# Attention maps combined before they are turned, latent heads and keys made in pairs, and small steps placed between output chunks

## The chip, the cores and the metric

One core of one Trainium2 chip. The metric is the device time of one execution in microseconds; the kernel is launched once and computes everything in fp32.

## The reference

One inference step of a two-layer network for 128 context tokens and 128 latent tokens (D = 1024). Each layer has a token mixer and a mixture of 64 experts. Cut to what the change touches:

```python
# differential attention, 4 heads of 32+32: for each head
a = softmax(q1 @ k1.T * scale) - lam * softmax(q2 @ k2.T * scale)
o_d = a @ v                                   # (tokens, 64) a head; then rmsnorm over the 64
# latent attention, 8 heads
kv = ckv_all @ w_ukv                          # k_nope and v of every head, 64 + 64
s = q_nope @ k_nope.T + q_rope @ k_rope.T
o_m = softmax(s * scale) @ v                  # (tokens, 64) a head
# retention, 4 heads, in both directions; its output is gated by silu(rg)
mix = concatenate([ret_out, diff_out, mla_out], -1)     # 256 + 256 + 512
x = x + gate1 * (mix @ w_out)
x = x + gate2 * moe_ffn(h)                    # 64 experts, top 6, and a shared one
```

## The kernel before

The activations lie turned in SBUF: xT, hT and mixT have channels on the partitions and the 256 tokens (128 context, 128 latent) in the free dimension. Instructions are written by hand for every engine, in one order that is fixed by the text, and the engines wait for each other by semaphores (names in `S[...]`). The order of the code in the block of an engine is therefore the order of its queue.

A layer is: norm, mixer, norm, experts. The weights of the mixer arrive in pieces of up to 2 MB through a ring of four slots (`gu`): SyncE issues the load of piece n when piece n - 4 is used (`weights_used`). Pieces are five of w_in, w_uq and w_ukv together (`mla`), two of w_out, the shared expert's, and pieces of w_ada, the modulation, which are multiplied at the places that `ADA_AT` names (16 of 2 MB in layer 0, 8 in layer 1) and gathered in `rada`. After the mixer the 64 experts go through 22 rounds a layer, 3 MB of weights for each expert. TensorE's block takes the ada pieces up as small matrix products (`ada`), and after each four a selection (`ada_select`), whose result VectorE adds up (`ada`, L975).

Attention runs in six units i a layer (`UNITS`). Units 0, 1, 2 are differential: 0 is all heads of the context (8 maps of 128 keys), 1 and 2 are two heads each of the latent tokens (4 maps of 256 keys). Units 3, 4, 5 are latent attention: 3 the context's 8 heads, 4 and 5 four heads each with 256 keys. A map lies with the queries on its partitions. The steps of a unit are:

- scores (TensorE, L1541 or L1551), into the two PSUM banks of the unit;
- `negated_max` (VectorE, L1031), then `exps` (ScalarE, L764), which leave the exponentials in `prob` and their sums;
- `turns` (TensorE, L1555): eight 128 x 128 transposes of `prob`. All transposes of the mixer have the line of the helper `turn`, L1440;
- `even_half` (VectorE, L1039) and `odd_half` (ScalarE, L771) copy the turned maps to `probT`;
- `values` (TensorE, L1577): eight products with the turned map as the stationary weights and 64 columns of values moving through;
- `results` (VectorE, L1043): reciprocals of the sums, the scaling (L1052 or L1056), and for the differential units the subtraction of the second maps with `nlam`, squares and their sums. `o_done` frees the banks.

Latent keys: L1667, one product for each of eight heads, 64 wide weights (w_ukv) and 384 columns moving, each into partitions 0 to 63 of a bank of its own; ScalarE copies each (L834). Behind them come three products for the values, `vm` (L1675).

The mixer's end on TensorE is, in order: the last ada piece, `ada_select` (L1458, waits for `rada`), the retention's cross products (`ret_x`, L1722), four turns of keys (`t_k`), `turn_mix` for the blocks 1, 2 and 3 of `mix` (each four turns; block 1 is the differential heads', 2 and 3 the latent heads'), the retention's products (`ret_o`, L1747), its state (`kv_p`, L1753), and the output projection `project_out` (L1762), in eight chunks c of 128 output channels, each a sum over eight k blocks of `mixT`. Block 0 of `mix`, the retention's, is ready last, so its turns stand between chunks. A norm's sum over the partitions (L1484) is a product with a matrix of ones, and four idle products (L1493) follow it.

The profile gives an fp32 product as two instructions.

## Time and profile before

| what | value |
|---|---|
| median of 3 runs | 1385.82 us (1382.41 to 1386.05) |
| the profiled execution | 1387.04 us, its span 1385.2 us |
| TensorE, matmul busy | 1256.7 us (91%) |
| VectorE, ScalarE busy | 276.8 us (20%), 233.9 us (17%) |
| DMA queue q1, share of 16 engines | 86.9%, 492.68 MB |
| mean granted TensorE clock | 0.965 of full |
| layer 0: mixer with its norm, experts | about 33 to 206 us, 232 to 703 us |
| layer 1: mixer with its norm, experts | about 703 to 872 us, 898 to 1385 us |

Times in the views are microseconds from the span's start. The 1.84 us between the span and the time of the execution lie outside the profile. An engine's busy share is an average over stages with different limits, so the stages are read one by one.

### The profile page before, as it was taken

How to read it: one execution, taken by the hardware profiler on the slowest of the kernel's cores; microseconds unless marked ns; L12 is line 12 of the kernel's file. 1: busy time of each engine (PE TensorE's matmuls, PEld its weight loads, DVE VectorE, ACT ScalarE, POOL GpSimd, SP SyncE). 2: the span in 40 equal slices, each digit the busy share in tenths (PEclk: the TensorE clock that was granted, in tenths of full speed). 3: DMA queues.
4: the chain of work that ended last, by engine and by line, in shares of the span. 5: the costliest groups of instructions: out<-in, count | busy, mean ns of one | idle time of the engine just before them, and what ended most of it. 6: DMA issues, size and time to landing. Idle time of an engine off the chain costs nothing.

```text
span 1385.2 us, 22873 instructions
## 1 busy us (share of the span) xinstructions
PE 1256.7 (91%) x9680; PEld 860.7 (62%) x9680; DVE 276.8 (20%) x696; ACT 233.9 (17%) x516; POOL 2.7 (0%) x13
## 2 busy tenths in 40 slices
PE   4999999999998898888999999999999789888976
PEld 2566687667666565646565668766767465555644
DVE  2142244111110110101033424511011010101012
ACT  2143213110100000000133421311000001000101
POOL 0000000000000000000000000000000000000000
PEclk9999999999999999999999999999999999999998
DMA  9886639899999999999956554899999999999990
GB/s 391 343 337 252 267 128 407 354 421 421 420 421 421 421 423 422 422 422 421 396 190 254 206 200 160 366 367 418 421 421 420 421 422 422 422 421 423 421 409 35
DMA packets 81025, 496.16 MB, mean 358 GB/s; under 512 B 10560, under 2 KB 12864, under 8 KB 24640
## 3 DMA queue, kind: packets, MB, share of 16 engines
q1 hardware_dynamic: 76752, 492.68, 86.9%
q10 hardware_dynamic: 4208, 2.52, 0.6%
q8 instruction: 52, 0.85, 0.2%
q14 instruction: 13, 0.11, 0.0%
HBM read 493.17 MB, written 2.00 MB: 357 GB/s over the span
## 4 chain that ended last, share of the span: by engine, by line
PE 67%; DMA 28%; DVE 2%; SPq 1%; ACT 1%; issue 1%; DVEq 0%; ACTq 0%
DMA dn<-in_exp_w_down 18%; PE PS L1909 14%; PE PS L1938 12%; PE PS L1503 8%; PE PS L1841 7%; PE PS L1848 7%; DMA gu<-in_exp_w_gate 5%; PE PS L1762 4%; DMA gu<-in_w_in 2%; PE PS L1440 2%; PE PS L1807 2%; PE PS L1471 2%; DMA gu<-in_w_ada 2%; PE PS L1577 1%; PE PS L1885 1%
## 5 line engine op out<-in xcount | busy, mean ns | idle before, releaser
L1909 PE MATMUL PS<-gu,arena 128*32 128x256 f32 (+1 forms) x3072 | 319.6, 383 | 1.8 <-issue 1.8
L1909 PEld LDWEIGHTS PS<-gu,arena 128*32 128x32 f32 (+1 forms) x3072 | 187.4, 118 | 79.8 <-issue 19.8
L1938 PE MATMUL PS<-arena 128*64 128x512 f32 (+1 forms) x336 | 174.3, 667 | 60.8 <-DMA dn<-in_exp_w_down 59.3
L1938 PE MATMUL PS<-dn,arena 128*32 128x512 f32 (+1 forms) x688 | 182.1, 631 | 0.0
L1841 PE MATMUL PS<-arena 128*128 128x128 f32 x1408 | 176.3, 278 | 0.5 <-ACT arena L923 0.5
L1841 PEld LDWEIGHTS PS<-arena 128*128 128x128 f32 x1408 | 164.1, 192 | 17.9 <-issue 16.7
L1848 PE MATMUL PS<-arena 128*128 128x256 f32 x704 | 159.6, 380 | 1.4 <-ACT arena L905 1.4
L1909 PE MATMUL PS<-arena 128*64 128x256 f32 (+1 forms) x672 | 151.9, 379 | 0.0
L1848 PEld LDWEIGHTS PS<-arena 128*128 128x128 f32 x704 | 130.4, 190 | 19.8 <-ACT arena L905 3.2
L1358 DVE TENSOR_TENSOR arena<-arena,PS 128x256 f32<-128x256 f32 x44 | 18.5, 421 | 564.1 <-ACT arena L919 564.1
L905 ACT ACTIVATE arena<-PS 128x512 f32<-128x512 f32 x88 | 52.6, 597 | 458.5 <-PE PS L1938 458.5
L1938 PEld LDWEIGHTS PS<-arena 128*64 128x64 f32 (+1 forms) x336 | 43.4, 140 | 112.7 <-issue 109.9
L1909 PE MATMUL PS<-xh,arena 128*64 128x256 f32 x352 | 86.8, 403 | 25.0 <-DMA gu<-in_exp_w_gate 21.2
L1909 PEld LDWEIGHTS PS<-arena 128*64 128x64 f32 (+1 forms) x672 | 83.4, 124 | 20.4
L1909 PEld LDWEIGHTS PS<-xh,arena 128*64 128x64 f32 x352 | 49.3, 145 | 64.0 <-DMA gu<-in_exp_w_gate 25.0
L1938 PEld LDWEIGHTS PS<-dn,arena 128*32 128x32 f32 (+1 forms) x688 | 47.4, 126 | 45.6 <-issue 42.8
L1352 DVE COPY arena<-PS 128x512 f32<-128x512 f32 x44 | 30.4, 691 | 214.5 <-PE PS L1440 214.5
L919 ACT ACTIVATE arena<-PS 128x256 f32<-128x256 f32 x44 | 16.9, 384 | 325.1 <-PE PS L1909 325.1
L1503 PE MATMUL PS<-gu,xh 128*128 128x512 f32 (+1 forms) x192 | 66.0, 498 | 1.5 <-DMA gu<-in_w_in 1.5
L1503 PE MATMUL PS<-xh,gu 128*128 128x256 f32 x256 | 58.2, 388 | 3.0 <-DVE xh L1006 1.7
L1503 PEld LDWEIGHTS PS<-xh,gu 128*128 128x128 f32 x256 | 49.2, 194 | 12.4 <-DMA gu<-in_w_in 4.0
L1762 PE MATMUL PS<-xh,gu 128*128 128x256 f32 x256 | 56.1, 380 | 0.0
(232 smaller groups left out, 989.1 us busy)
## 6 DMA issues: line engine op xcount, KB each, us to landing
gu<-in_exp_w_gate SPq DMA_DIRECT2D x106, 1024.0 KB, 16.3
gu<-in_exp_w_up SPq DMA_DIRECT2D x86, 1024.0 KB, 17.6
dn<-in_exp_w_down SPq DMA_DIRECT2D x86, 1024.0 KB, 18.3
gu<-in_w_ada SPq DMA_DIRECT2D x24, 2048.0 KB, 10.8
arena<-in_exp_w_up SPq DMA_DIRECT2D x42, 1024.0 KB, 14.8
arena<-in_exp_w_down SPq DMA_DIRECT2D x42, 1024.0 KB, 16.8
xh<-in_exp_w_gate SPq DMA_DIRECT2D x22, 1024.0 KB, 11.3
gu<-in_w_in SPq DMA_DIRECT2D x8, 2048.0 KB, 12.6
```

The costliest lines, as they stand in the source:

```text
L905: return A(yy[:, :, half], PS[:, 7 - n, :].rearrange("p (t c) -> p c t", c=NC_), ACT.Copy)
L1352: return v.tensor_copy(turned_back, PS[:, 6, :])
L1358: tt(hh, sact, PS[:, 5, FF:2 * FF], ALU.mult).then_inc(S["hid_ready"], 1)
L1440: return pe.transpose(dst, src, ident[0:parts, 0:parts])
L1471: ins = mmul(PS[32 * j:32 * j + 32, 7, :], condw[:, 2 * quarter + c, :], wv[:, c, 512 * j:512 * j + 512], start=(quarter == 0 and c == 0), ...
L1503: ins = mmul(PS[0:lhs(k).shape[-1], bank, o:o + rhs(k).shape[-1]], lhs(k), rhs(k), start=(k == 0), stop=(k == NC_ - 1))
L1762: ins = mmul(PS[:, wo_bank(c), (c % 2) * T:(c % 2) * T + T], wo[k // 4][:, k % 4, c], mixT[:, k], start=(first and k == ks[0] and c in (0, ...
L1807: ins = mmul(PS[:, bank, j * T:j * T + T], w[:, u, k, j], hT[:, k, :], start=(k == 0), stop=(k == NC_ - 1))
L1841: ins = mmul(PS[:, 4, (c % 4) * P:(c % 4) * P + P], h_tok[:, g, c], onehot[b][:, g], start=(g == 0), stop=(g == 1))
L1848: ins = mmul(PS[:, c // 2, (c % 2) * T:(c % 2) * T + T], yy[:, c], selT, start=(first and c % 2 == 0), stop=False, skip_group_check=True)
L1909: ins = mmul(PS[w * h:w * h + w, 5, FF * half:FF * half + FF], xg[:, k, w * h:w * h + w], weights[half][:, k], start=(k == 0), stop=(k == ...
L1938: ins = mmul(PS[w * h:w * h + w, 7 - n, :], hidT[:, j * P + w * h:j * P + w * h + w], weights[:, j, 512 * n:512 * n + 512], start=(j == 0) ...
```

## The change

What it does, part by part:

- **Differential maps are combined first.** `combined` (VectorE) makes the reciprocals, a factor for each head (sum of the first map times the reciprocal of the second's, times `nlam`), and adds the second map of a pair, times the factor, to the first, in place in `prob`. A unit then has four blocks to turn instead of eight and four products instead of eight; one ScalarE copy of a bank (`turned_maps`) takes the place of `even_half` and `odd_half`; `results` scales the heads directly.
- **Latent values.** `scaled` (VectorE) multiplies the maps by the reciprocals before they are turned. `values` for units 3 to 5 takes 64 columns of `vm` as stationary weights and moves 128 columns of the turned map; two heads are written to partitions 0 to 63 and 64 to 127. The result is turned already: `latent_results` copies it to `latent_T`, which `project_out` reads for k = 4 to 7. `turn_mix(2)` and `turn_mix(3)` are gone.
- **Latent keys.** Two heads at once, into the two halves of the partitions of one bank; one `ukv_k` and one wait for a pair.
- **The mixer's end.** `ada_select`, the turns of keys, and kv_p stand between output chunks 0 to 4, and so does the wait for `ada_mod`; on VectorE the addition for `ada`, the decayed keys and `dk_tok` stand behind the retention's result; on ScalarE the retention's root stands ahead of the copy of the state.

The diff, cut:

```diff
--- before.py
+++ after.py
...
+                def turned_maps(i):
+                    act.wait_ge(S["dt_turned"], 3 * l + i + 1)
+                    A(probT[:, i % 2, 0:4], PS[:, unit_bank(i), :].rearrange("p (t q) -> p t q", t=4),
+                      ACT.Copy).then_inc(S["dt_out"], 1)
...
                 for h in range(MLA_H):
-                    act.wait_ge(S["ukv_k"], MLA_H * l + h + 1)
-                    A(kmT[0:64, h], PS[0:64, k_bank(h), 0:3 * P].rearrange("p (k t) -> p k t", k=3),
+                    if h % 2 == 0:
+                        act.wait_ge(S["ukv_k"], 4 * l + h // 2 + 1)
+                    at = 64 * (h % 2)
+                    A(kmT[0:64, h], PS[at:at + 64, k_bank(h // 2), 0:3 * P].rearrange("p (k t) -> p k t", k=3),
                       ACT.Copy).then_inc(S["km_a"], 1)
...
+                def scaled(i):
                     n = maps_of(i)
                     v.wait_ge(S["exp_done"], U0 + i + 1)
                     link(v.reciprocal(unit_small(i, INV_SUM), unit_small(i, SUM)))
+                    maps = prob[:, i % 2].rearrange("p (j k) -> p j k", j=n)
+                    tt(maps, maps, bc(unit_small(i, INV_SUM), 2, 8 * P // n), ALU.mult).then_inc(S["p_scaled"], 1)
+                    settle("p_scaled")
+                def latent_results(i):
                     v.wait_ge(S["pv_done"], U0 + i + 1)
...
+                    n = maps_of(i) // 2
+                    at, tokens = (2 if i == 5 else 0), (slice(0, P) if i == 3 else slice(P, T))
+                    v.tensor_copy(latent_T[:, at:at + n, tokens], PS[:, unit_bank(i), 0:P * n].rearrange("p (k t) -> p k t", k=n)
+                                  ).then_inc(S["o_done"], 1)
...
+                def combined(i):
+                    n = maps_of(i)
+                    w = 8 * P // n
+                    v.wait_ge(S["exp_done"], U0 + i + 1)
+                    sums, inv, factor = unit_small(i, SUM), unit_small(i, INV_SUM), unit_small(i, MAX)[:, 0:n // 2]
+                    link(v.reciprocal(inv, sums))
+                    link(tt(factor, sums[:, 0:n:2], inv[:, 1:n:2], ALU.mult))
+                    link(ts(factor, factor, nlam[:, l:l + 1], None, ALU.mult))
+                    maps = prob[:, i % 2].rearrange("p (j k) -> p j k", j=n)
+                    for h in range(n // 2):
+                        ins = stt(maps[:, 2 * h], maps[:, 2 * h + 1], factor[:, h:h + 1], maps[:, 2 * h], ALU.mult, ALU.add)
+                    ins.then_inc(S["p_scaled"], 1)
+                    settle("p_scaled")
+                def results(i):
+                    n = maps_of(i)
+                    v.wait_ge(S["pv_done"], U0 + i + 1)
+                    heads, at = (od[:, 0], 470) if i == 0 else (od[:, 1, 128 * (i - 1):128 * i], 472 + 2 * i)
+                    tt(heads.rearrange("p (h e) -> p h e", e=DIF_V),
+                       PS[:, unit_bank(i), 0:32 * n].rearrange("p (h e) -> p h e", e=DIF_V),
+                       bc(unit_small(i, INV_SUM)[:, 0:n:2], 2, DIF_V), ALU.mult).then_inc(S["o_done"], 1)
...
+                combined(0)
                 negated_max(1)
-                even_half(0)
                 ada_lag(l, "P2", "P3")
+                combined(1)
...
-                even_half(1)
                 negated_max(2)
                 results(1)
-                even_half(2)
+                combined(2)
...
+                scaled(3)
+                scaled(4)
...
                 negated_max(5)
+                scaled(5)
...
-                v.wait_ge(S["t_mix"], 4 * l + 4)
-                v.tensor_copy(mixT[:, 0:2, :], PS[:, 4, :].rearrange("p (k t) -> p k t", k=2)).then_inc(S["mixT_d"], 1)
+                ada(ADA_BY[l] - 1)
+                v.wait_ge(S["t_k"], l + 1)
+                for d in range(2):
...
                 def turns(i):
-                    pe.wait_ge(S["exp_done"], U0 + i + 1)
+                    pe.wait_ge(S["p_scaled"], U0 + i + 1)
+                    if i < 3:
+                        w = 8 * P // maps_of(i)
+                        for n in range(4):
+                            at = n * P // w * 2 * w + n * P % w
+                            ins = turn(PS[:, unit_bank(i), n * P:n * P + P], prob[:, i % 2, at:at + P])
+                        ins.then_inc(S["dt_turned"], 1)
+                        return
...
+                    else:
+                        for pair in range(maps_of(i) // 2):
+                            for k in range(nk):
+                                for j in (2 * pair, 2 * pair + 1):
+                                    h = j + (4 if i == 5 else 0)
+                                    at = 64 * (j % 2)
+                                    ins = mmul(PS[at:at + 64, unit_bank(i), pair * P:pair * P + P],
+                                               vm[:, k if i == 3 else k + 1, 64 * h:64 * h + 64],
+                                               probT[:, i % 2, j * nk + k], start=(k == 0), stop=(k == nk - 1))
...
-                for h in range(MLA_H):
-                    if h == 1:
+                for b in range(MLA_H // 2):
+                    if b == 1:
                         pe.wait_ge(S["o_done"], U0 + 2)
-                    if h == 2:
+                    if b == 2:
                         pe.wait_ge(S["kpe_roped"], l + 1)
-                    if h >= 3:
-                        pe.wait_ge(S["km_a"], MLA_H * l + h - 2)
-                    mmul(PS[0:64, k_bank(h), 0:3 * P], w_ukv[:, 128 * h:128 * h + 64],
-                         ckvT.rearrange("p k t -> p (k t)"), start=True, stop=True).then_inc(S["ukv_k"], 1)
+                    if b == 3:
+                        pe.wait_ge(S["km_a"], MLA_H * l + 2)
+                    for h in (2 * b, 2 * b + 1):
+                        at = 64 * (h % 2)
+                        ins = mmul(PS[at:at + 64, k_bank(b), 0:3 * P], w_ukv[:, 128 * h:128 * h + 64],
+                                   ckvT.rearrange("p k t -> p (k t)"), start=True, stop=True)
+                    ins.then_inc(S["ukv_k"], 1)
...
-                ada_select(ADA_BY[l] - 1)
...
-                for c in range(2):
-                    turn(PS[:, 3, c * P:c * P + P], kT[:, c, 0:P])
-                for c in range(2):
-                    ins = turn(PS[:, 3, (2 + c) * P:(3 + c) * P], dkT[:, c, 0])
-                ins.then_inc(S["t_k"], 1)
...
                 pe.wait_ge(S["dif_normed"], l + 1)
-                pe.wait_ge(S["ada_mod"], ADA_BY[l])
-                turn_mix(1, 6)
-                turn_mix(2, 7)
-                pe.wait_ge(S["o_done"], U0 + 6)
-                turn_mix(3, 2)
+                turn_mix(1, 3)
...
+                others, theirs = (4, 5, 6, 7, 2, 3), (0, 1)
+                pe.wait_ge(S["cross_ready"], l + 1)
+                pe.wait_ge(S["o_done"], U0 + 6)
+                pe.wait_ge(S["mixT_a"], l + 1)
+                project_out(0, others, True, False)
+                project_out(1, others, True, False)
+                ada_select(ADA_BY[l] - 1)
+                project_out(2, others, True, False)
+                for c in range(2):
+                    turn(PS[:, 2, c * P:c * P + P], kT[:, c, 0:P])
+                for c in range(2):
+                    ins = turn(PS[:, 2, (2 + c) * P:(3 + c) * P], dkT[:, c, 0])
+                ins.then_inc(S["t_k"], 1)
+                project_out(3, others, True, False)
                 pe.wait_ge(S["ktok_ready"], l + 1)
...
                 ins.then_inc(S["kv_p"], 1)
...
                 pe.wait_ge(S["ret_mixed"], l + 1)
-                pe.wait_ge(S["kv_ready"], l + 1)
-                turn_mix(0, 4)
-                project_out(3, (4, 5, 6, 7, 2, 3), True, False)
-                pe.wait_ge(S["mixT_d"], 2 * l + 2)
+                turn_mix(0, 5)
+                project_out(4, others, True, False)
+                pe.wait_ge(S["mixT_d"], l + 1)
                 for c in range(NC_):
-                    if c < 4:
-                        ins = project_out(c, (0, 1), False, True)
+                    if c < 5:
+                        ins = project_out(c, theirs, False, True)
                     else:
-                        ins = project_out(c, (4, 5, 6, 7, 2, 3, 0, 1), True, True)
+                        if c == 6:
+                            pe.wait_ge(S["ada_mod"], ADA_BY[l])
+                        ins = project_out(c, others + theirs, True, True)
                     if c == NC_ - 1:
...
```

Two places where the order of the queues moves. In these rows a line number is the program's own (before.py ahead of the change, after.py behind it), a product counts once where the profile gives two instructions, and `arena`, `xh`, `dn`, `small` are the SBUF tensors that the names above lie in: `prob` and `mixT` in `xh`, `probT` in `dn`, `latent_T` in `arena`.

VectorE, from the norm of the latents to the decay factors. Before (L1047 to L1073 is `results(0)`, L1039 `even_half`, L1031 and L1033 `negated_max(2)`, L1047 to L1073 again `results(1)`):

```order
L1047 RECIPROCAL small<-small 128x8
L1056 TENSOR_TENSOR arena<-PS,small 128x512
L1070 SCALAR_TENSOR_TENSOR arena<-arena,nlam 128x2x64 x2
L1072 TENSOR_TENSOR arena<-arena 128x256
L1073 TENSOR_REDUCE small<-arena 128x4
L975 TENSOR_TENSOR mod<-PS,cst 128x32
L1039 COPY dn<-PS 128x512
L1031 TENSOR_REDUCE small<-PS 128x2x2
L1033 TENSOR_SCALAR small<-small 128x4
L1047 RECIPROCAL small<-small 128x4
L1056 TENSOR_TENSOR arena<-PS,small 128x256
L1070 SCALAR_TENSOR_TENSOR arena<-arena,nlam 128x128
```

Now (L1088 to L1093 `results`, L1074 to L1076 the start of `combined(2)`, whose two fused operations of 256 columns, L1079, follow):

```order
L1088 TENSOR_TENSOR arena<-PS,small 128x256
L1092 TENSOR_TENSOR arena<-arena 128x256
L1093 TENSOR_REDUCE small<-arena 128x4
L982 TENSOR_TENSOR mod<-PS,cst 128x32
L1038 TENSOR_REDUCE small<-PS 128x2x2
L1040 TENSOR_SCALAR small<-small 128x4
L1088 TENSOR_TENSOR arena<-PS,small 128x128
L1092 TENSOR_TENSOR arena<-arena 128x128
L1093 TENSOR_REDUCE small<-arena 128x2
L1074 RECIPROCAL small<-small 128x4
L1075 TENSOR_TENSOR small<-small 128x2
L1076 TENSOR_SCALAR small<-small,nlam 128x2
```

The reciprocal and the subtraction are gone from `results(0)`, the copy ahead of the maximum is gone, and the maps of unit 2 are combined behind `results(1)`.

TensorE, from the last ada piece to the output chunks. Before (L1471 the ada piece, L1458 the selection, L1762 `project_out`):

```order
L1471 MATMUL PS<-gu,condw 32x512 x8
L1458 MATMUL PS<-cst,rada 128x4x2 x4
L1722 MATMUL PS<-late,dn 128x128 x4
L1440 MATMUL PS<-cst,dn 128x128 x2
L1440 MATMUL PS<-cst,arena 128x128 x14
L1747 MATMUL PS<-dn 128x64 x8
L1753 MATMUL PS<-dn 64x64 x8
L1762 MATMUL PS<-xh,gu 128x256 x18
L1440 MATMUL PS<-cst,arena 128x128 x4
L1762 MATMUL PS<-xh,gu 128x256 x46
```

Now (L1490 ada, L1477 the selection, L1784 `project_out`, L1808 kv_p):

```order
L1490 MATMUL PS<-gu,condw 32x512 x8
L1759 MATMUL PS<-late,dn 128x128 x4
L1459 MATMUL PS<-cst,arena 128x128 x4
L1774 MATMUL PS<-dn 128x64 x8
L1784 MATMUL PS<-arena,gu 128x256 x4
L1784 MATMUL PS<-xh,gu 128x256 x2
L1784 MATMUL PS<-arena,gu 128x256 x4
L1784 MATMUL PS<-xh,gu 128x256 x2
L1477 MATMUL PS<-cst,rada 128x4x2 x4
L1784 MATMUL PS<-arena,gu 128x256 x4
```

and on from there:

```order
L1784 MATMUL PS<-xh,gu 128x256 x2
L1459 MATMUL PS<-cst,dn 128x128 x2
L1459 MATMUL PS<-cst,arena 128x128 x2
L1784 MATMUL PS<-arena,gu 128x256 x4
L1784 MATMUL PS<-xh,gu 128x256 x2
L1808 MATMUL PS<-dn 64x64 x8
L1459 MATMUL PS<-cst,arena 128x128 x4
L1784 MATMUL PS<-arena,gu 128x256 x4
```

Sixteen turns in a row have become four ahead of the first chunk, four behind the third and four behind kv_p; the selection stands behind the second chunk.

## Rows read from the trace of the kernel before

**Rows 1.** Stages: us, busy us of each engine (instructions), granted clock, DMA share, GB/s.

```profile
121.40:169.00 47.60, 47.51 (x264) 31.37 (x264) 8.53 (x18) 9.47 (x21) 0.00 (x0) 1.00 0.75 283
...
232.30:703.00 470.70, 427.33 (x3734) 289.67 (x3735) 55.72 (x119) 47.89 (x88) 0.00 (x0) 0.96 1.00 413
...
898.00:1385.20 487.20, 431.59 (x3752) 293.45 (x3752) 62.80 (x132) 51.38 (x97) 0.00 (x0) 0.95 0.94 389
```

**Rows 2.** The chain of waits through the mixer of layer 0: start, us, what.

```profile
85.29 0.12 DVE small L1047
...
85.43 0.70 DVE arena L1056
...
88.94 1.24 DVE small L1031
...
90.41 1.93 ACT xh L764 x8
...
92.61 0.26 ACT arena L815
...
104.91 5.30 PE PS L1667 x16
...
113.11 8.29 DMA gu<-in_w_in
...
139.35 1.73 PE PS L1577 x16
...
157.22 1.09 PE PS L1710 x16
...
171.38 1.90 PE PS L1440 x16
...
175.00 1.08 PE PS L1753 x16
```

**Rows 3.** TensorE in order of time: start, us, what [idle before <- its end].

```profile
17.84 1.92 PE L1471 MATMUL PS<-gu,condw 128*32 128x512 f32 x16 [1.05 <-DMA gu<-in_w_ada]
22.81 3.41 PE L1471 MATMUL PS<-gu,condw 128*32 128x512 f32 x16 [3.04 <-DMA gu<-in_w_ada]
...
86.61 0.70 PE L1541 MATMUL PS<-arena 32*128 32x256 f32 x4
...
88.46 1.97 PE L1641 MATMUL PS<-arena,gu 128*96 128x256 f32 x8
...
92.92 1.97 PE L1641 MATMUL PS<-arena,gu 128*96 128x256 f32 x8 [0.76 <-ACT arena L815]
...
121.45 7.17 PE L1503 MATMUL PS<-xh,gu 128*128 128x256 f32 x32 [1.28 <-DMA gu<-in_w_in]
...
169.67 1.06 PE L1458 MATMUL PS<-cst,rada 128*128 128x8 f32 x8 [0.72 <-ACT rada L729]
...
206.24 0.74 PE L1484 MATMUL PS<-xh,cst 128*128 128x256 f32 x2 [1.90 <-DVE xh L1240]
...
232.30 7.13 PE L1909 MATMUL PS<-gu,arena 128*64 128x256 f32 x64 [0.90 <-issue]
...
757.61 0.70 PE L1541 MATMUL PS<-arena 32*128 32x256 f32 x4 [0.71 <-DVE arena L1056]
```

**Rows 4.** VectorE in order of time, layer 0.

```profile
83.76 0.88 DVE L1122 SCALAR_TENSOR_TENSOR arena<-arena,small,late 128x256 f32<-128x256 f32 x2
...
88.22 0.69 DVE L1039 COPY dn<-PS 128x512 f32<-128x512 f32 x1 [0.31 <-DVE mod L975]
...
180.49 0.69 DVE L1227 TENSOR_TENSOR arena<-arena 128x512 f32<-128x512 f32 x1
```

**Rows 5.** SyncE's queue in order of time, one issue.

```profile
76.67 0.47 SPq L603 DMA_DIRECT2D gu<-in_mla_w_ukv  x1
```

**Rows 6.** DMA issues between 76.5 and 78: KB each, us to landing.

```profile
gu<-in_mla_w_ukv SPq DMA_DIRECT2D x1, 512.0 KB, 11.1
```

**Rows 7.** ScalarE in order of time, one copy of the latent keys.

```profile
105.73 0.48 ACT L834 ACTIVATE arena<-PS 64x384 f32<-64x384 f32 x1 [3.24 <-PE PS L1667]
```

126 lines of the change are left out of this document (46 added, 80 removed).

## The prediction, made before the changed kernel ran

> **What bounds the kernel now.** I read the stage table first. In the two expert stretches the DMA engines are busy all or nearly all of the time (share 1.00 and 0.94), in the mixer stretch they are not (0.75) while TensorE is busy 47.51 of 47.60 us [rows 1]. So an expert stretch lasts as long as its weights need, and it starts when the mixer of its layer ends. Nothing in the diff changes what the expert part loads or computes, and its loads are released by the mixer's last steps (`weights_used` of the w_out pieces, `order_ready`). A microsecond taken out of a mixer's path moves the rest forward by one.
>
> Second view, the chain of waits through layer 0's mixer: nearly all pieces are TensorE's, one behind the other, with two exceptions, a stretch on VectorE and ScalarE that ends with the third exponentials at 92.34 and the copy behind them (92.61), and a load of w_in at 113.11 [rows 2]. Third, TensorE in order of time: it waits 0.76 us for that copy, 1.28 for the load, 0.72 for `rada`, 1.90 for the sums of squares at the end [rows 3]. So the sum is one of TensorE's work, except before 92.92, where a chain of other engines decides.
>
> **Prices.** A turn costs 1.90/16 = 0.12 us. Eight value products (16 instructions, 64 columns moved, 128 wide weights) cost 1.73, so 0.108 an instruction. The eight key products cost 5.30 [rows 2].
>
> *Differential units (0, 1, 2).* Per unit 4 turns and 4 products go: 0.48 + 0.87. On units 0 and 1 that is 2.7 us a layer of TensorE work, but the path there is: the last w_in piece, ScalarE's roots, VectorE's norms, the first product of `results(0)` (`o_done`), scores of unit 2, their maximum, four exponentials, two copies, `queries(1)`. On it I count, in layer 0: 0.48 for the turns of unit 0 ahead of the piece; 0.40 in `results(0)`, whose reciprocal (0.12 and a gap) has been made earlier and whose multiply is 256 wide instead of 512 (0.70 to about 0.44, half of the 256 wide pair of L1122) [rows 2, 4]; 0.48 because TensorE came to the scores at 86.61 though `o_done` stood at 86.13, and now has 1.3 us less to do ahead of them; 0.48 because the maximum, ready to start at 88.46, started at 88.94 behind `even_half(1)` (0.69), whose copy is now ScalarE's [rows 2 to 4]. Sum 1.8. In layer 1 TensorE already waited 0.71 for `o_done` [rows 3], so the third item falls away: 1.3. The query weights of layer 0 are issued at 76.67 and land 11.1 later, at 87.8 [rows 5, 6], so TensorE will wait about 0.7 us there before `queries(0)`; that costs nothing, since it has 1.3 us to spare before `queries(1)`.
>
> *What `combined` adds.* A reciprocal, two tiny operations and two to four fused ones: 3 x 0.2 (estimated from the reciprocal of 0.12 and its gaps) + 2 x 0.44 + gaps = 1.6 us of VectorE before the turns. For units 0 and 1 other work of TensorE covers it (7 us of projection, then the ada products). For unit 2 it stands behind `results(1)` (three operations on 128 columns, under 0.44 each, about 1.0) after exponentials that end 1.8 us sooner, at 90.5: done at 93.1, while TensorE comes to the turns at 92.9. I charge 0.3 in layer 0, 0 in layer 1. Unit 2 itself gives 1.35. If the cover were gone, each unit would pay up to its 1.6.
>
> *Keys.* The program now writes two heads to the two halves of a bank, 64 wide weights each. No such pair with 384 columns is in the trace. The nearest row is the experts' first round, where pairs of 64 wide weights moving 256 columns end every 7.13/64 = 0.111 us, against 7.17/32 = 0.224 for a 128 wide product of the same 256 columns [rows 3]: the halves run together. By that 5.30 becomes 2.65; from above it stays 5.30. I take the pair: it is the same form. ScalarE still makes eight copies of 0.48 [rows 7], which took turns with products every 0.66; now they get two at a time. If they don't overlap they need 3.84, and TensorE's third vm product waits for the first vm copy (512 columns, by the same row 0.6): 0.66 + 3.84 + 0.6 = 5.1 us after the start, against 2.65 + 2 x 0.9 = 4.5 for TensorE (four times 0.224 a product). Below, they overlap and cost 0. I take 0 and keep 0.6 a layer for the range. The Trainium skill, TensorEngine Tiling (Array Packing), section PSUM Bottleneck, says of this case that tiling speeds up TensorE but not the copies out of PSUM, which may then decide; by it the forecast would be 1.2 us later in all. `km_rows` on VectorE comes out level with TensorE's scores (both 5.5 earlier); no charge.
>
> *Latent values.* Weights are now 64 columns of vm, 128 columns of maps move, again in pairs. No row has it. From above: no overlap, half of 0.224 an instruction, 1.79 against 1.73, nothing gained (-0.06). From below: half of 0.111, 0.89. Between them lie two near rows: 128 columns moved in alternating row halves, 1.09 for 16, and 64 wide weights with 64 columns, 1.08 for 16 [rows 2]. I take 1.09: 0.64 saved, three units a layer, 1.9. `scaled` adds a multiply over 1024 elements on VectorE (1.24, as the maximum over 1024 took [rows 2], and a reciprocal). It stands before turns(3), (4) and (5), and all three lie behind a projection of 7 us; free.
>
> *Tail.* Turning of blocks 2 and 3 is gone: 8 x 0.12 = 0.95. The wait of 0.72 for `rada` goes, since two output chunks stand ahead of the selection. ret_x, the four turns of the differential block and the retention products (16 instructions of 64 columns, 1.7) now take under 3 us; the copies needed for the first chunk (`mixT_a`, `cross_ready`) are done before their end. Late next would be `ret_mixed`: the retention chain takes 6.2 us after `ret_o` (175.00 to 181.18 [rows 2, 4]), and TensorE reaches its turns 13 us after it, behind four chunks of 12 instructions of 0.224 (2.7 each), the selection (1.06 [rows 3]), four turns and kv_p. `ktok_ready`: three operations 256 wide after t_k, 1.3 at most, covered by chunk 3 (2.7). Stores leave some 2 us later and land before VectorE's third chunk; the end stays TensorE's last chunk and the 1.90 behind it. Sum 1.7 a layer.
>
> *The load of w_in, piece 0, in layer 0* is issued when `mla` is used, 8.29 before it lands [rows 2]. Both move together, so the 1.28 stays.
>
> **Sum.** Layer 0: 1.8 + 1.0 + 2.65 + 1.9 + 1.7 = 9.1. Layer 1: 1.3 + 1.35 + 2.65 + 1.9 + 1.7 = 8.9. Together 18.0. The profiled execution took 1387.04; 1369.0 follows. The median of the three runs lies 1.2 below it: **1367.8**. A measurement of this kernel tells a change from none at about 0.3%, 4.2 us.
>
> **Rivals.**
> 1. *The halves don't run together* in the new places (keys and values alternate after a wait, or the bank serialises them). Keys and latent values give nothing: 18.0 - 5.3 - 3.8 = 8.9, time 1377. For: no row has exactly this form. Against: the experts' round does it 64 times in a row in one bank.
> 2. *New waits take a part back*: the key copies (0.6 a layer), `combined(2)` up to 1.6 a layer, one wait in the tail: about 4 us, time 1372. For: by the working above VectorE and ScalarE come out within 0.5 us of TensorE at three places. Akin to it: the loads of layer 0 decide all before 121 us, and its 5.5 are lost: 1373. Against: the one load that TensorE waits for there is issued only when TensorE frees its slot, at 113.11.
> 3. *Slower.* TensorE's clock. After a wait of 3.04 us at the start 16 ada instructions take 3.41 instead of 1.92 [rows 3], a factor 1.78, as if most of them ran at the lower of its two levels (1.2 and 2.4 GHz). If the longer waits before `queries(0)` and `queries(1)` and the half wide weights brought it down for the attention stretch, 50 us of TensorE work a layer, with half of that at the lower level in both layers, 50 x 0.78 = 39 us would be added: 1407. It decides from 28 us of such work on (28 x 0.78 = 18 + 4.2). Against: waits of 0.76 and 1.28 left no mark, the stage after them has the full clock [rows 1].
>
> **How the numbers follow.** Forecast with its bounds (all values at 0.89: 1.2 less; runs spread by 3.6): 1363 to 1372, chance 0.66. Rival 2: 0.17. Rival 1: 0.12. Rival 3: 0.02; unforeseen 0.03. The range 1363 to 1377 takes in rivals 1 and 2 and holds about nine tenths by these cases, of which I keep eight, as the unknown prices are mine. Faster by over 0.3%: 0.93; within: 0.04; slower: 0.03.
>
> **What would show it.** Keys: 16 instructions in about 2.7 us. Latent values: 1.1, differential values 0.87 for 8. TensorE's wait before `queries(1)` grows to about 1.3 in layer 1. No wait at the selection. w_in's wait stays near 1.3. The mixer from 70.35 to the norm's sum is 9 us shorter in both layers, and the expert stretches last 470.7 and 487.2 us as before. Pairs that take 5.3 and 1.8 prove rival 1; a granted clock under 1.0 between 70 and 165 us rival 3; expert stretches that grow by what the mixers lose would make the ground of the sum wrong.

## The result, and the profile after

The changed kernel takes 1364.92 us (median of 3 runs, 1364.84 to 1365.53) against 1385.82 before: a ratio of 0.9858, 95% interval 0.9834 to 0.9882. The forecast was 1367.8 with a range of 1363 to 1377. The profiled execution took 1364.92 us with a span of 1362.9; before it was 1387.04 and 1385.2, so the spans differ by 22.3 us. TensorE is busy 1233.8 us instead of 1256.7, VectorE 283.2 instead of 276.8, ScalarE 232.4 instead of 233.9.

The stages first (us; busy us and instructions of TensorE, weight loads, VectorE, ScalarE, GpSimd; granted clock; DMA share; GB/s). They are a part of the changed kernel's mixer, from the same 121.40 as in [rows 1] to its last ada piece, and the two stretches that each start with the first expert product; the first of them ends with the next layer's first product of w_in:

```profile
121.40:162.60 41.20, 41.20 (x248) 24.43 (x246) 9.55 (x17) 9.21 (x20) 0.00 (x0) 1.00 0.74 274
223.87:702.79 478.92, 435.80 (x3776) 296.23 (x3777) 62.97 (x139) 53.52 (x98) 1.01 (x4) 0.97 0.99 410
879.85:1362.90 483.05, 427.52 (x3752) 292.04 (x3752) 62.64 (x131) 51.34 (x97) 0.00 (x0) 0.96 0.95 392
```

They answer to [rows 1], but are cut elsewhere: the first expert stretch there ended at 703.00, 9.79 us ahead of the first product of w_in, so 478.92 is to be set against 480.49 (below), not against 470.70. The mixer is still TensorE's (busy all of the 41.20 us), the expert stretches still belong to the DMA engines. TensorE in order of time, changed kernel (start, us, what, [idle before <- its end]), answers to [rows 3]:

```profile
91.49 1.97 PE L1675 MATMUL PS<-arena,gu 128*96 128x256 f32 x8 [1.33 <-ACT arena L822]
93.29 0.60 PE L1459 MATMUL PS<-cst,xh 128*128 128x128 f32 x4
...
102.08 2.83 PE L1704 MATMUL PS<-arena,gu 128*64 128x384 f32 x16
104.84 1.98 PE L1713 MATMUL PS<-gu,arena 128*128 128x512 f32 x4
107.73 1.12 PE L1713 MATMUL PS<-gu,arena 128*128 128x512 f32 x2 [0.91 <-DVE arena L1180]
108.69 3.68 PE L1570 MATMUL PS<-arena 96*128 96x128 f32 x24
...
117.12 7.17 PE L1522 MATMUL PS<-xh,gu 128*128 128x256 f32 x32 [1.18 <-DMA gu<-in_w_in]
...
134.95 1.09 PE L1610 MATMUL PS<-dn,arena 128*64 128x128 f32 x16
135.97 1.09 PE L1459 MATMUL PS<-cst,xh 128*128 128x128 f32 x8
...
170.68 0.95 PE L1477 MATMUL PS<-cst,rada 128*128 128x8 f32 x8
...
198.19 0.70 PE L1503 MATMUL PS<-xh,cst 128*128 128x256 f32 x2 [1.90 <-DVE xh L1259]
```

The keys (L1704) go from 5.30 us to 2.76 (102.08 to 104.84). The latent values (L1610) take 1.02 us to the next instruction instead of 1.73 [rows 2], three times a layer. The selection at 170.68 waits for nothing; before it waited 0.72. The load of w_in still costs 1.18. The 1.90 before the norm's sum stays. Two waits are of interest: the one before `queries(1)` is now 1.33 (0.76 before), and 1.36 in layer 1, where about 1.3 was forecast; the one of 0.91 before the third vm product is **new**, and it was not in the sum.

With the starts of such rows the mixers can be cut into pieces whose ends are the same instruction in both kernels. Layer 0 starts with the second piece of w_in (53.79 before, 54.02 after), layer 1 with its first (712.79, 702.79); both end with the first product of the norm's sum.

| piece, layer 0 | before | after | gain | forecast |
|---|---|---|---|---|
| start to `queries(1)` | 53.79 to 92.92 | 54.02 to 91.49 | 1.66 | 1.8 |
| `queries(1)` to the keys | to 104.84 | to 102.08 | 1.33 | 1.0 |
| keys and vm, to the scores of unit 3 | to 112.92 | to 108.69 | **1.47** | **2.65** |
| scores of unit 3 to w_in's piece | to 121.45 | to 117.12 | 0.10 | 0 |
| to the last ada piece (latent values) | to 167.03 | to 160.72 | 1.98 | 1.9 |
| tail | to 206.24 | to 198.19 | 1.74 | 1.7 |
| sum | 152.45 | 144.17 | 8.28 | 9.1 |

In layer 1 the same pieces give 1.56, 1.33, 1.47, 1.84 (w_in's piece has no wait there) and 1.74, together 7.94 (159.32 to 151.38), against 8.9. So the mixers give 16.2 us, 1.8 less than forecast. One row, the keys' with the vm products, is 2.4 short in the two layers; the others together gave 0.6 more than their forecast. Yet the span is 22.3 shorter. The other 6.1 us lie where nothing was forecast:

| stretch | before | after | gain |
|---|---|---|---|
| norms between mixer and experts, both layers | 26.06 + 26.05 | 25.68 + 25.68 | 0.75 |
| experts of layer 0 (first expert product to first w_in product) | 480.49 | 478.92 | 1.57 |
| experts of layer 1 (first expert product to the end) | 487.04 | 483.05 | 3.99 |
| start | 53.79 | 54.02 | -0.23 |

Two questions are left for experiments: what holds the third vm product, and why the last expert stretch, where the programs are alike, is 4 us shorter. The diffs below are cut, and where a step is long they name it in words.

### The profile page after: what moved, and what is told of

It reads as the page before. It is cut to its first block, busy times and chain, and to the rows that moved or that the text cites. A ratio compares the mean times of both kernels' runs of the same rounds, so it can differ in the third digit from the quotient of the medians.

```text
span 1362.9 us, 22695 instructions
## 1 busy us (share of the span) xinstructions
PE 1233.8 (91%) x9592; PEld 842.0 (62%) x9592; DVE 283.2 (21%) x714; ACT 232.4 (17%) x514; POOL 2.7 (0%) x13
## 4 chain that ended last, share of the span: by engine, by line
PE 64%; DMA 29%; DVE 2%; SPq 2%; issue 2%; ACT 1%; DVEq 0%
DMA dn<-in_exp_w_down 19%; PE PS L1948 14%; PE PS L1977 12%; PE PS L1522 8%; PE PS L1880 7%; PE PS L1887 6%; DMA gu<-in_exp_w_gate 6%; PE PS L1784 4%; DMA gu<-in_w_in 2%; PE PS L1490 2%; PE PS L1846 2%; PE PS L1459 2%; DMA gu<-in_w_ada 2%; PE PS L1924 1%; SPq L500 1%
## 5 line engine op out<-in xcount | busy, mean ns | idle before, releaser
L1948 PE MATMUL PS<-gu,arena 128*32 128x256 f32 (+1 forms) x3072 | 316.3, 382 | 1.8 <-issue 1.8
L1948 PE MATMUL PS<-xh,arena 128*64 128x256 f32 x352 | 83.8, 393 | 24.9 <-DMA gu<-in_exp_w_gate 24.9
L1522 PE MATMUL PS<-xh,gu 128*128 128x256 f32 x256 | 58.4, 389 | 2.4 <-DVE xh L1013 1.2
L1490 PE MATMUL PS<-gu,condw 128*32 128x512 f32 x384 | 47.7, 622 | 6.3 <-DMA gu<-in_w_ada 5.7
```

The costliest lines, as they stand in the source:

```text
L1490: ins = mmul(PS[32 * j:32 * j + 32, 7, :], condw[:, 2 * quarter + c, :], wv[:, c, 512 * j:512 * j + 512], start=(quarter == 0 and c == 0), ...
L1522: ins = mmul(PS[0:lhs(k).shape[-1], bank, o:o + rhs(k).shape[-1]], lhs(k), rhs(k), start=(k == 0), stop=(k == NC_ - 1))
L1948: ins = mmul(PS[w * h:w * h + w, 5, FF * half:FF * half + FF], xg[:, k, w * h:w * h + w], weights[half][:, k], start=(k == 0), stop=(k == ...
```

## The experiments

Stages below are read from each profile as above: mixer 0, mixer 1, last stretch. For the changed kernel they are 144.17, 151.38, 483.05. Both kernels were run again, to see how far a stage moves by itself.

**before_again** and **after_again**, both unedited.

> The kernel before, unchanged, once more. Question: of the 22.3 us between the two profiled spans 16.2 lie in the two mixers, 0.8 in the norms behind them and 5.6 in the expert stretches, which I had taken as equal; 4.1 of these are the last expert round of layer 1, where the gate and up products of the kernel before took 8.81 us and stood 2.59 behind the landed weights, against 7.13 and 0.14. Theory A (chance of a single execution): the expert stretches of this second profile differ from the first by some us, the last round takes 7.1 in some executions, and this kernel's own times spread over 3 to 4 us (1382 to 1386). Theory B (the change shortens the expert part too): the second profile repeats 487.0 us from the first expert product of layer 1 to the end, within 1 us, and the last round again takes 8.8.

> The changed kernel, unchanged, once more, on the chip of before_again. Theory A: the time is 17 to 22 us under that of the kernel before, and the mixers (first product of the second w_in piece to the sum of squares in layer 0, first w_in product to it in layer 1) repeat 144.2 and 151.4 us within 0.3, while the expert stretch of layer 1 may differ from 483.1 by up to 4 us. Theory B: that stretch repeats 483 within 1 us.

Measured: 1385.09 (1383.39 to 1388.56, 10 runs), ratio 0.9998 (0.9988 to 1.0008), stages 152.41, 159.32, 485.94; and 1365.52 (4 runs), ratio 0.9854 (0.9838 to 0.9871), stages 144.66, 151.37, 482.75. The mixers repeat within 0.5 us. The 0.49 by which mixer 0 of the change is longer in its repeat comes in here (TensorE in order of time, after_again):

```profile
88.42 1.97 PE L1675 MATMUL PS<-arena,gu 128*96 128x256 f32 x8 [0.95 <-DMA gu<-in_mla_w_ukv]
91.55 1.97 PE L1675 MATMUL PS<-arena,gu 128*96 128x256 f32 x8 [0.33 <-ACT arena L822]
93.91 0.66 PE L1459 MATMUL PS<-cst,xh 128*128 128x128 f32 x4 [0.39 <-DVE xh L1079]
```

The query weights land later here, so the values of unit 1 and behind them `results(1)` and `combined(2)` (L1079) are late, and the turns of unit 2 wait 0.39, which the first profile doesn't have. The last stretch of before lies at 486 to 487, that of the change at 483, so this difference is no accident of one profile. The norms are not a gain: 25.67 and 26.06 both occur with either program (before_again has 25.67 and 25.68, rows_first 26.06 and 25.67). Layer 0's experts are worth 0.2 to 2.0 us: 479.12 in before_again, 478.49 in after_again. Between the two repeats the spans differ by 19.1 us, not 22.3: 15.7 in the mixers, 3.2 in the last stretch, 0.6 in layer 0's experts, and 0.4 lost in the start.

**values_one_half**: do the two halves of the partitions run together?

```diff
-    for k in range(nk):
-        for j in (2 * pair, 2 * pair + 1):
...
-            at = 64 * (j % 2)
+    for j in (2 * pair, 2 * pair + 1):
+        for k in range(nk):
...
+            at = 0
```

> The changed kernel with the latent value products all written to partitions 0 to 63, one head's over the other's, so neighbouring products no longer alternate between the two halves (half of the latent heads' results are left out). Same count, same weights width, same columns. Theory (the halves run together): the 16 instructions of a unit take 1.8 us or somewhat more instead of 1.02, three units a layer, so 0.8 x 6 = 4.7 us more, 1369.6. Rival (they are short because their weights are only 64 wide, not because of the halves): they stay at 1.0 to 1.1 and the time at 1365.

Measured: TensorE in order of time, this kernel, the latent values of unit 3:

```profile
135.24 1.96 PE L1610 MATMUL PS<-dn,arena 128*64 128x128 f32 x16
137.13 1.09 PE L1459 MATMUL PS<-cst,xh 128*128 128x128 f32 x8
```

From start to start 1.89 us instead of 1.02, the same sixteen instructions. With alternating halves they end every 0.064 us, in one half every 0.118. In unit 3 a head has one block of keys, so the order of the loops changes nothing there and the half alone makes the difference. So the halves do run together, and rival 1 falls for the values. (Two heads also write over one another here; in keys_single, next, each has a bank of its own, and products in one half take the long time all the same.) (What this kernel leaves out changes the routing, and the branch for overflowing experts, which the others skip, is taken; the total of 4435 us says nothing, only the first mixer is read.)

**keys_single**: one key product at a time, as before, all else as changed.

```diff
-    for b in range(MLA_H // 2):
-        for h in (2 * b, 2 * b + 1):
-            at = 64 * (h % 2)
-            mmul(PS[at:at + 64, k_bank(b), ...])
+    for h in range(MLA_H):
+        mmul(PS[0:64, k_bank(h), ...])
```

> The changed kernel with the latent keys made one head at a time as before, in a bank each. Theory (two halves run together): the key products take 5.3 instead of 2.76 us; the wait of 0.91 ahead of the third vm product, which I put down to ScalarE's eight copies in a row, goes, so the net loss is 2.54 - 0.91 = 1.6 us a layer, 3.3 in all, 1368.2. Rival (that wait is for VectorE's rows copy, which ends at the same moment): the same 1.6, since both are covered by slower keys; what would differ is told by value_copy_first and rows_first. Rival (no overlap of copies and products matters): 5.1 us in all, 1370.

Measured: 1369.72, ratio 0.9884 (0.9864 to 0.9903); stages 145.79, 152.86, 483.03. TensorE in order of time:

```profile
103.68 5.37 PE L1700 MATMUL PS<-arena,gu 128*64 128x384 f32 x16
108.99 2.94 PE L1708 MATMUL PS<-gu,arena 128*128 128x512 f32 x6
111.76 3.68 PE L1568 MATMUL PS<-arena 96*128 96x128 f32 x24
```

The three vm products, six instructions, stand in one row without a wait. From the keys to the scores 8.08 us, as before, against 6.61 with pairs. The pairs save 2.54 us of products, and 1.07 comes back in the vm products, net 1.47. So rival 1 falls for the keys too. The mixers are 1.1 to 1.6 and 1.5 longer. The medians differ by more, 4.2 us from after_again and 4.8 from the first three runs; in the one profile of this kernel 1.6 us lie in its start, which reaches the second w_in piece at 55.63 instead of 54.02, and what made it late is not known.

**What holds the third vm product?** The profile names VectorE's copy of the key rows (L1180). But two things end there within 0.05 us. ScalarE and, below, VectorE, of the changed kernel in order of time:

```profile
102.99 4.06 ACT L843 ACTIVATE arena<-PS 64x384 f32<-64x384 f32 x8 [2.37 <-PE PS L1704]
107.08 1.08 ACT L850 ACTIVATE arena<-PS 128x512 f32<-128x512 f32 x2
```

```profile
105.96 1.75 DVE L1180 COPY arena<-arena 32x3072 f32<-32x3072 f32 x1
```

The eight key copies take 4.06 us, 0.51 each from start to start and 0.48 busy, so they don't overlap; the first vm copy (0.60) ends at 107.68. The row copy ends at 107.71. The product starts at 107.73. In the code the third vm product waits for the bank that the first vm copy frees; the row copy is wanted by the scores behind it. Two kernels tell them apart.

**value_copy_first**: ScalarE copies the first vm bank after six of the eight keys. **rows_first**: VectorE's row copy stands ahead of `results(2)`.

```diff
 # value_copy_first, ScalarE
-    eight key copies
-    three value copies
+    key_copies(range(6))
+    value_copy(0)
+    key_copies((6, 7))
+    value_copy(1)
+    value_copy(2)
 # rows_first, VectorE
-    results(2)
     v.tensor_copy(kmT[64:96], ...).then_inc(S["km_rows"], 1)
+    results(2)
```

> The changed kernel; ScalarE copies the first vm product ahead of the last two key copies. Theory S (the 0.91 us wait ahead of the third vm product is for ScalarE, whose eight key copies take 4.06 us): the wait goes, the latent scores start as soon as the third product is done and VectorE's rows copy has ended, 0.8 to 0.9 us sooner, 1.7 us in all, 1363.2. Theory V (the wait is for VectorE's rows copy, as the profile's releaser says): the third vm product still waits until 107.7 and nothing is gained, 1364.9.

> The changed kernel; VectorE makes the rows copy ahead of results(2), about 1 us sooner. Theory S: nothing, 1364.9, the wait of 0.91 stays with ScalarE's copy as its cause. Theory V: the wait shrinks by all of its 0.9 us in each layer, 1363.1.

Measured (4 runs each): value_copy_first 1363.91, ratio 0.9843 (0.9818 to 0.9868), stages 143.53, 150.58, 482.86; rows_first 1364.99, ratio 0.9845 (0.9820 to 0.9870), stages 144.15, 151.37, 483.08. The medians can't tell them apart; the rows can. ScalarE of value_copy_first, then TensorE of value_copy_first, then VectorE and TensorE of rows_first, each in order of time:

```profile
103.20 3.04 ACT L844 ACTIVATE arena<-PS 64x384 f32<-64x384 f32 x6 [2.37 <-PE PS L1711]
106.26 0.60 ACT L852 ACTIVATE arena<-PS 128x512 f32<-128x512 f32 x1
```

```profile
105.04 2.99 PE L1720 MATMUL PS<-gu,arena 128*128 128x512 f32 x6
```

```profile
104.89 1.75 DVE L1179 COPY arena<-arena 32x3072 f32<-32x3072 f32 x1
```

```profile
107.62 1.13 PE L1713 MATMUL PS<-gu,arena 128*128 128x512 f32 x2 [0.90 <-ACT arena L850]
```

With the vm copy sooner the three products run in one piece, keys to scores in 5.74 us (102.28 to 108.02) instead of 6.61. With the row copy ended 1.1 us sooner nothing changes but the name that the profile gives. So it is the first vm copy that the product waits for, and what makes that copy late is the eight key copies ahead of it.

**latent_copies_first**: can the wait of 1.33 before `queries(1)` be had? ScalarE does the two copies that it waits for ahead of the exponentials of unit 2.

```diff
-    exps(2)
     A(ckvT[:, 0:3:2, :], ...)
     A(kpeT[0:MLA_QK, 0:3:2, :], ...)
+    exps(2)
```

> The changed kernel; ScalarE makes the copies of the turned latents (ckvT, kpeT) ahead of the third exponentials, which they don't need. In the changed kernel TensorE waits 1.33 us (layer 0) and 1.36 (layer 1) for them ahead of queries(1). Theory (that wait is an order on ScalarE): it goes, but the next one comes at once: the exponentials end 0.5 us later, so combined(2) ends 93.3 and the turns of unit 2, now due at 92.0, wait 1.3 us; net 0 to 0.4 us a layer, 1364 to 1365. Rival (the wait is all there is): 2.7 us in all, 1362.2.

Measured: 1364.65, ratio 0.9855 (0.9835 to 0.9875); stages 143.81, 150.95, 483.18. TensorE in order of time:

```profile
90.05 1.92 PE L1675 MATMUL PS<-arena,gu 128*96 128x256 f32 x8
92.90 0.66 PE L1459 MATMUL PS<-cst,xh 128*128 128x128 f32 x4 [0.93 <-DVE xh L1079]
```

The wait before `queries(1)` is gone, and one of 0.93 stands before the turns of unit 2, where VectorE's `combined(2)` (L1079) is now late. The net is 0.4 to 0.8 in layer 0 and 0.4 in layer 1, about what the first theory said, and not the 2.7 of its rival. So `combined` does cost something as soon as its cover is taken away, here by TensorE that comes sooner and by exponentials that come later: in the change it ended at 92.79 and TensorE came at 93.29.

**maps_not_combined**: the differential units in their old form (eight turns, eight products, `even_half`, `odd_half`, `results` with the subtraction).

```diff
-    combined(i); turned_maps(i)
+    even_half(i); odd_half(i)
...
-    for j in range(maps_of(i) // 2):
+    for j in range(maps_of(i)):
```

> The changed kernel with its differential units as before: eight turns, eight products, two copies, the subtraction on the results. All else stays. Theory (my sum: a chain of VectorE and ScalarE sets the path up to queries(1), TensorE's work behind it): the stretch up to the latent keys is longer by 3.0 us in layer 0 and 2.9 in layer 1 as measured between the two kernels, so 5.9 us in all, 1370.8. Rival (all TensorE work that goes is time): three units of 1.35 us a layer, 8.1 us, 1373. Rival (the latent keys wait for VectorE or ScalarE anyway, and take it back): the 0.9 us wait ahead of the third vm product shrinks to 0, and only about 4 us are lost, 1369.

Measured: 1375.04, ratio 0.9922 (0.9902 to 0.9942); stages 147.18, 153.87, 487.36. Combining is worth 2.5 to 3.0 us in mixer 0 and 2.5 in mixer 1, so 5.0 to 5.5 where the theory said 5.9, the rivals 8.1 and 4. But the medians (2 runs here) lie 9.5 to 10.1 apart and the time missed the theory's 1370.8: 4.3 of that is the last stretch again, behind everything that was edited.

**tail_order_before**: the small steps in front of the output projection again, the latent turns still gone.

```diff
+    ada_select(ADA_BY[l] - 1)
     ret_x
+    turns of keys (t_k)
...
+    kv_p
     project_out(0 .. 3)
-    (the same steps between its chunks)
```

VectorE's part of these steps moves with them; the later wait for `ada_mod` and ScalarE's earlier root stay as in the change.

> The changed kernel with the selection, the four turns of keys and the retention's state ahead of the first output chunk as before (latent_T and the removed turns stay changed). Theory: only the wait of 0.7 us for rada comes back, in each layer, 1.4 us in all, 1366.3; the same instructions stand elsewhere. Rival (small steps between chunks cover more: ktok_ready, mixT_a or the retention's root come late in the old order once the eight turns are gone): 1 to 2 us more a layer, 1368 to 1370. Rival (they cover nothing): 1364.9.

Measured: 1367.02, ratio 0.9863 (0.9831 to 0.9896); stages 144.99, 152.24, 482.62. The wait for `rada` is back with its old size (TensorE in order of time):

```profile
163.46 1.06 PE L1477 MATMUL PS<-cst,rada 128*128 128x8 f32 x8 [0.72 <-ACT rada L730]
```

Layer 1 has it too, at 820.11. The mixers are 0.3 to 0.8 and 0.9 longer: the placing is worth that wait of 0.72 within the spread of a mixer, and no more can be told from it.

**after_skip_longer** and **before_skip_shorter**: the last stretch. First what the profiles show there. The chain of waits ahead of the last of the 22 expert rounds (start, us, what), in before:

```profile
1331.97 15.54 DMA gu<-in_exp_w_gate
1347.51 2.59 issue
1350.10 8.81 PE PS L1909 x64
```

and in the changed kernel:

```profile
1313.22 16.11 DMA gu<-in_exp_w_gate
1329.34 0.14 issue
1329.47 7.13 PE PS L1948 x64
```

The weights land alike, 449.35 and 449.49 us after the first expert product. Then before waits for nothing that the profile shows, 2.59 us from the landing on (an idle time of 3.65), and the 64 instructions of the round's gate and up products take 8.81 instead of 7.13, at a granted clock of 0.54 from 1350.10 to 1352.00, 0.59 to 1354.00 and 1.00 behind. In maps_not_combined it is 3.20 from the landing on (idle 4.20), with 8.72. In before_again the weights were there 0.3 us before TensorE had finished the round ahead, and it stood idle for 2.29 all the same, with 7.13 behind. In every kernel with combined maps whose branch is neither edited nor taken the round starts 0.14 behind the landing, after an idle time of 0.61 to 1.77 that ends with it. Ahead of the last round of each layer TensorE's program jumps over a branch for overflowing experts, which isn't taken. The change takes 88 instructions out of the matmul count (9680 to 9592) and as many weight loads, 72 of the 88 by the combined maps (9664 without), so what stands behind the jump lies elsewhere in the stream. That made a theory; both kernels change only the text inside the branch that isn't taken.

```diff
 # after_skip_longer, inside the branch, both layers
+    for k in range(9 if w == 0 else 0):
+        mmul(..., over_xg[:, 0], both[:, :, 0], start=True, stop=True)
 # before_skip_shorter, inside the branch, both layers
-    for k in range(NC_):
+    for k in range(1 if w == 0 else 4):
```

> The changed kernel, with nine products repeated in the first window of TensorE's overflow branch, in the program text of both layers; the branch is not taken here, so nothing more is executed, but everything behind it stands 72 + 72 instructions later in TensorE's stream, as in the kernel whose maps were not combined. Theory F (the wait of TensorE ahead of the last expert round, 2.3 to 4.2 us that the profile calls issue, comes from where the code behind the skipped branch stands in the instruction stream): the stretch from the first expert product of layer 1 to the end lasts 486 to 487 us instead of 483, with an issue wait of 2 to 4 us ahead of the last round, time 1368 to 1369. Rival G (it comes from the timing of the run, what the kernel does ahead of it, and the position doesn't matter): 483, no issue wait over 1 us, time 1365.

> The kernel before, with 11 of the 16 gate and up products of the overflow branch left out in the program text of both layers (the branch is not taken here, so nothing less is executed); what stands behind it comes 88 + 88 instructions sooner in TensorE's stream, so about where it stands in the changed kernel. Theory F: the last stretch lasts 483 us instead of 486 to 487, no issue wait over 1 us ahead of the last round, time 1381 to 1382. Rival G: as before, 486 to 487 with an issue wait of 2.3 to 3.7 us, time 1385.

Measured: after_skip_longer 1366.81 (1366.61 to 1367.10), ratio 0.9865 (0.9841 to 0.9888), stages 144.43, 152.59, 483.73; before_skip_shorter 1383.54 (10 runs), ratio 0.9988 (0.9977 to 0.9999), stages 152.28, 159.31, 484.64. The chain of waits at the same place, after_skip_longer and then before_skip_shorter:

```profile
1330.00 2.30 PE PS L1948 x18
1332.30 0.65 issue
1332.95 5.34 PE PS L1948 x46
```

```profile
1345.12 0.14 issue
1345.26 0.83 PE PS L1909 x5
1346.09 1.70 issue
1347.79 6.69 PE PS L1909 x59
```

Neither theory comes out with its number. The wait without a releaser is **moved** by text that is never executed: from ahead of the round to behind its 5th instruction in before_skip_shorter, and out of nowhere to behind the 18th in after_skip_longer. So the place of the code in the stream does matter, which rival G excludes; but 0.7 to 1.0 us was added where theory F said 3 to 4, and 1.3 to 2.4 taken away where it said 3 to 4. (Mixer 1 of after_skip_longer is 1.2 us longer too; that is the clock, see the last section.)

The sizes that the expectations give to the two shifts, 72 + 72 and 88 + 88 instructions, are twice too large. values_one_half, where one branch runs, has 2048 matmul instructions for its 64 x 2 x 8 gate and up products, two for each, and as many weight loads. Nine products in the text of both layers are then 36 and 36, eleven are 44 and 44, and neither kernel puts the last round where the other program has it. Sorted by how many matmul instructions fewer stand ahead of it than in before (weight loads change by the same number, other instructions are not counted), the wait moves into the round and gets shorter:

| kernel | fewer matmul instructions | the wait of TensorE |
|---|---|---|
| before, before_again | 0 | ahead of the round, idle 3.65, 2.29 |
| maps_not_combined | 16 | ahead of the round, idle 4.20 |
| before_skip_shorter | 44 | behind the 5th instruction, 1.70 |
| after_skip_longer | 52 | behind the 18th, 0.65 |
| the change and the other kernels with its maps | 88 | none |

The profile also counts DMA queues of the kind "instruction". In before, from 1345.90 to 1350.20 (packets, MB, share of 16 engines):

```profile
q8 instruction: 1, 0.02, 1.5%
```

Narrower windows put the start of this packet at 1347.31, so TensorE's round starts 2.79 us behind it. The thirteen kernels, all but values_one_half, each have one such packet here. Where the wait stands ahead of the round, it ends 2.78 to 2.80 us behind the packet's start (before, before_again, maps_not_combined); where it stands within the round, 2.37 and 2.42 behind (before_skip_shorter, after_skip_longer). Where there is no wait, the packet starts between 0.52 us ahead of the round and 0.75 behind its start, and the products run on. The idle times of the first three differ by 1.9 us, and this distance by 0.02, so the wait is tied to the loading of instructions. What sets the packet off and which instructions it holds is not shown, and how long a wait will be can't be told beforehand from the shift.

**combined_best**: value_copy_first and latent_copies_first and rows_first together, and on TensorE the ada piece ahead of the turns of unit 2.

```diff
     queries(1)
-    turns(2)
     ada_here(ada, l, "UQ")
+    turns(2)
```

> The changed kernel with four moves and no other work: the latent copies ahead of the third exponentials, the turns of unit 2 behind the ada piece that followed them, the first vm copy ahead of the last two key copies, the rows copy ahead of results(2). Theory: no wait ahead of queries(1) (1.3 us a layer), none ahead of the turns, none ahead of the third vm product (0.9), the scores of unit 3 right behind it: 2.2 us a layer, but the decay chain on VectorE moves with the exponentials and may take 0.3 back: 4.0 us in all, 1360.9. Rival (VectorE's chain to the rows copy becomes the bound, since it moves only with kpe_rot): 2 us in all, 1363.

Measured: 1361.45 (1359.26 to 1363.94, 4 runs), ratio 0.9823 (0.9805 to 0.9841); stages 141.97, 150.45, 483.08. It beats both kernels: its slowest run, 1363.94, lies under the fastest of the changed kernel's seven, 1364.38. Mixer 0 is 2.2 to 2.7 us shorter than in the changed kernel: no wait before `queries(1)`, before the turns or in the vm products. Mixer 1 has none of these waits either, but gains only 0.9. The stages of this kernel around its query products of layer 1 (us, busy us of TensorE, granted clock, DMA share, GB/s):

```profile
743.80:746.80 3.00, 2.64 (x16) 0.94 1.02 429
746.80:750.10 3.30, 3.30 (x10) 0.54 1.02 432
750.10:754.00 3.90, 3.90 (x29) 1.00 0.37 155
```

The eight instructions of `queries(0)` took 3.46 us instead of 1.97 at a granted clock of 0.54, so near the lower of the two levels (1.2 GHz of 2.4). These 1.5 us are most of what is missing.

| kernel | us | ratio to before (95%) | mixer 0 | mixer 1 | last stretch |
|---|---|---|---|---|---|
| before_again | 1385.09 | 0.9998 (0.9988 to 1.0008) | 152.41 | 159.32 | 485.94 |
| after_again | 1365.52 | 0.9854 (0.9838 to 0.9871) | 144.66 | 151.37 | 482.75 |
| keys_single | 1369.72 | 0.9884 (0.9864 to 0.9903) | 145.79 | 152.86 | 483.03 |
| maps_not_combined | 1375.04 | 0.9922 (0.9902 to 0.9942) | 147.18 | 153.87 | 487.36 |
| tail_order_before | 1367.02 | 0.9863 (0.9831 to 0.9896) | 144.99 | 152.24 | 482.62 |
| value_copy_first | 1363.91 | 0.9843 (0.9818 to 0.9868) | 143.53 | 150.58 | 482.86 |
| rows_first | 1364.99 | 0.9845 (0.9820 to 0.9870) | 144.15 | 151.37 | 483.08 |
| latent_copies_first | 1364.65 | 0.9855 (0.9835 to 0.9875) | 143.81 | 150.95 | 483.18 |
| combined_best | 1361.45 | 0.9823 (0.9805 to 0.9841) | 141.97 | 150.45 | 483.08 |
| after_skip_longer | 1366.81 | 0.9865 (0.9841 to 0.9888) | 144.43 | 152.59 | 483.73 |
| before_skip_shorter | 1383.54 | 0.9988 (0.9977 to 0.9999) | 152.28 | 159.31 | 484.64 |

## Why the prediction was right, and where it wasn't

**What bounds the kernel.** Right. Every piece that left TensorE's path in a mixer moved all that follows, and the experts' loads moved with it.

**Differential units 0 and 1** (1.8 and 1.3 to `queries(1)`): 1.66 and 1.56. The path over VectorE and ScalarE was the right one to count, not the 2.7 us of TensorE's work: the wait before `queries(1)` grew to 1.33 and 1.36; for layer 1 about 1.3 was forecast. The wait forecast before `queries(0)` for the query weights came in the repeat of the changed kernel as 0.95 us and in two others as 0.41 (tail_order_before, combined_best), and in the first profile of the changed kernel not at all. It had been charged nothing, and up to `queries(1)` it costs nothing: that piece gives 1.67 in the repeat.

**Unit 2** (1.0 and 1.35): 1.33 in both layers of the first profile. The 0.3 charged for `combined(2)` in layer 0 was not needed there; it is done 0.5 us ahead of TensorE. In the repeat it was: TensorE waits 0.39 for it, and the piece gives 0.72. latent_copies_first too shows how thin that cover is.

**Keys** (2.65): 1.47. This is the term of the mixers that was mis-sized. The products came out as forecast, 2.54 less by alternating halves. What failed is "Below, they overlap and cost 0. I take 0": ScalarE's copies don't overlap, and the case from above held, nearly to its number. It was reckoned as 0.66 + 3.84 + 0.6 = 5.1 us from the first product to the third vm product's release against 4.5 for TensorE. Measured are 0.91 + 4.09 + 0.60 = 5.60 (102.08 to 107.68), each copy 0.51 from start to start instead of 0.48, against 4.74 for TensorE with its key products and the first two vm products. The wait of 0.91 and the restart behind it took 1.07 a layer back. value_copy_first shows it, rows_first excludes the other cause. By the Trainium skill, TensorEngine Tiling (Array Packing), section PSUM Bottleneck, the copies out of PSUM may decide once tiling has made TensorE four times as fast. The traces agree, and here twice as fast was enough: the products went from 5.30 us to 2.76, and the copies behind them take 4.06. By that rule the prediction reckoned 1.2 us later in all; measured are 2.1.

**Latent values** (1.9 a layer): 1.98 and 1.84 for their pieces. The row taken, 1.09 for sixteen, came out as 1.02 in the same measure, and values_one_half shows that without alternation it would have been 1.89, more than the 1.73 before, so no gain at all. `scaled` had its cover.

**Tail** (1.7 a layer): 1.74 and 1.74. No wait at the selection, none for `ktok_ready` or `ret_mixed`; the end stayed with TensorE's last chunk and 1.90.

**The load of w_in**: 1.18, taken as 1.28. It moved along.

**The expert stretches "last 470.7 and 487.2 us as before"**: wrong for the second, and it is the main reason why the total came out 2.9 us below the forecast though the mixers gave 1.8 less. The last stretch of before was longer by 4.0 us in the profiled pair and by 3.2 in the repeated one: a wait of TensorE behind the skipped branch, of 2.59 and 2.29 us, and in the first of the two products at a lower clock behind it (1.7). The change shifted that code and is rid of both. The prediction had no term for it and no view that would have priced it. So the forecast of the total is nearer than its sum deserved: two errors of opposite sign met, and that part of the agreement is luck.

**Rivals.** 1 (halves don't run together) fell by values_one_half and keys_single. 2 (new waits) was right in kind for the key copies, at 2.1 us in all instead of about 4, right for `combined(2)` in one profile of two, by 0.39 us, and wrong for the tail. 3 (the clock) did not come in the changed kernel, whose mixers have a granted clock of 1.00 from 54 to 198 us and from 702.8 to 854. In small it exists: see below.

## What to carry to other kernels

When TensorE's products are halved, divide the time by the engine that empties the banks: copies of 64 x 384 cost 0.51 us each here also when the products came two at a time, and a copy that frees a bank for waiting products belongs ahead of those that nobody waits for yet (0.9 us a layer for a moved line). Where two possible releasers end within 0.05 us, the one that the profile names is a guess: move each by itself. And compare the stretches that the edit does not touch too: text that is never executed moved one of them by 0.7 to 2.4 us here.
